# Dilated attention, product with V: V stationary instead of the probabilities, output turned back to rows by TensorE

## The chip, the cores and the metric

One program runs on one core of a Trainium2 chip. The metric is the device time of one execution in microseconds (us). The engines named below are TensorE (PE in the rows; its weight loads are PEld), VectorE (DVE), ScalarE (ACT), GpSimd (POOL) and SyncE (SP), which issues most of the loads. Lower is better.

## The reference, cut to what matters

The kernel computes two transformer-like blocks one after the other, for 1024 positions and 1024 features in float32. The change is in the second block, in its dilated attention: three groups of eight heads, each with its own stride between the positions that a query sees.

```python
DILATED_GROUPS = ((128, 1), (512, 4), (2048, 16))     # window, dilation
BLK, HEAD_DIM = 128, 64

def dilated_attention(q, k, v, window, dilation):
    ...
    qs = strided(q * (Dh ** -0.5))
    kb = with_prev(strided(k))          # own block of 128 keys and the one before
    vb = with_prev(strided(v))
    s = jnp.einsum('brnqhd,brnkhd->brnhqk', qs, kb, preferred_element_type=jnp.float32)
    ...
    m = jnp.max(s, axis=-1, keepdims=True)
    p = jnp.exp(s - m)
    den = jnp.sum(p, axis=-1)
    lse = m[..., 0] + jnp.log(den)
    o = jnp.einsum('brnhqk,brnkhd->brnqhd', p, vb.astype(jnp.float32))   # the product that changes
    o = o / jnp.swapaxes(den, -1, -2)[..., None]
    ...
    return o.astype(q.dtype), lse
```

## The kernel before

The kernel is a list of stages, each with a hand-written instruction sequence for every engine; semaphores (the `wait_ge` lines) order the engines against one another. Nothing reorders: what stands first in an engine's sequence runs first on it. The stage that is touched is `Dilated` (it fills the stretch from 1870 to 2480 us of the profiled execution).

It runs 12 units, i = 0 to 11. A unit is two heads of one group (group i % 3), with all 1024 positions in eight blocks of 128 queries, b = 0 to 7. A block looks at one or two chunks of 128 keys (`chunks`): in group 0 every block but the first has two, in group 1 the odd blocks have two, in group 2 all have one. Over the 12 units that makes 44 blocks with two chunks and 52 with one.

For a block, the work goes through the engines like this:

- `score` (PE, L2608 puts the mask in, L2610 adds the product of queries and keys, with 64 rows of the array for each head),
- `top` (DVE, L2503, the largest score of each row), `exps` (ACT, L2384, exponentials and their sums),
- `turn_p` (PE, L2627, transposes the probabilities of both heads, one or two chunks each), `take_turned` (ACT, L2394, copies them from PSUM to PT2),
- `value` (PE, L2639, the product with V into PSUM bank 7), `rows` (DVE, L2509 and L2512, row maximum and output to OS), `store` (POOL, L2447, to DRAM).

Into this are laid half tiles of the projection for the next units (`half_tile`, which calls `tile_part`: twelve matrix products of 128x512 at L319; in the last two units tiles of 24 products of 128x256 at L274). PE's order of one quarter q of a unit, with b = 2q, is: half tile; turn_p(b), score(b+2); half tile; **value(b), turn_p(b+1)**; half tile; **value(b+1), score(b+3)**, then for q < 2 the transposes of the next unit's V (`turn_v`, L2588), or for q >= 2 in every third unit those of a combined pair (`turn_pair`, L2273). Below, the first place in bold is called place A (48 times) and the second place B (48 times).

Other things that matter below: `v_rows` (ACT, L2369) copies the turned V out of the bank that turn_p(2) and turn_p(4) write next, so these wait for it; `pair_features` (ACT, L2279) does the same for the pair's bank, on which turn_p(6) waits in units 5, 8 and 11. In ACT's sequence both stand behind `exps(b+3)` and a split of weights (L258). DVE's sequence has `rows(b+1)` just ahead of `top(b+3)`. `value` of a block waits until DVE has copied the output of the block before, since there is one output place in PSUM.

`value` issues, for each head and chunk, one float32 product with the turned probabilities (128x128) as the stationary operand and V (128x64) as the moving one. Each is two instructions in the trace. The `Attention` stage of the first block (345 to 570 us) has a product of the other form, at L2123: V (64 columns) stationary, the turned probabilities (128 columns) moving, the two heads into the two halves of the output's partitions.

Of the kernel before, what the change touches and what calls it, by code (L numbers as in the profile page):

```python
# [16 lines left out]
F32 = mybir.dt.float32  # L17
# [3 lines left out]
ACT = mybir.ActivationFunctionType  # L21
AX = mybir.AxisListType.X

P = 128
# [3 lines left out]
HALF = 512  # L28
# [58 lines left out]
def hybrid_kernel(nc, A, out):  # L87
    ctx = ExitStack()
    with ctx:
# [42 lines left out]
        def phase(items):  # L132
# [49 lines left out]
        YC = phase([("below_yc", [P, 8, 512], F32), ("YC", [P, L], F32)])[1]  # L182
        (gv, XC, ct, cw, QR, KR, VF, PB2, V2, PT2, rt, rp, OS, mx2, mask_r) = phase(kept + [
            ("QR", [P, 2, L], F32), ("KR", [P, 2, L], F32),
            ("VF", [P, L], F32), ("PB2", [P, 2, 2, 256], F32),
            ("V2", [P, 2, 8, 2, HD], F32), ("PT2", [P, 2, 2, 2, P], F32),
            ("rt", [P, HALF], F32), ("rp", [P, HALF], F32), ("OS", [P, 2, 8, 2, HD + 2], F32),
            ("mx2", [P, 2, 16], F32), ("mask_r", [P, 4 * P], F32R)])
# [23 lines left out]
        gv_ready, gv_taken = sig("gate_v_tile_ready"), sig("gate_v_tile_taken")  # L212
        pair_loaded, pair_step, pair_exp = sig("head_pair_loaded"), sig("pair_step"), sig("pair_exponentials_ready")
        ct_turned, ct_taken = sig("combined_rows_turned"), sig("combined_features_taken")
        inverted, scale_rows, scale_taken = sig("row_sums_inverted"), sig("row_scales_spread"), sig("row_scales_taken")
# [109 lines left out]
        def first_tiles(pe, u, rows, ready):  # L325
# [4 lines left out]
            for half in range(2):  # L330
# [11 lines left out]
                for k in range(KT):  # L342
                    rows.turn(pe, half, k)
                    if k >= 2:
# [4 lines left out]
        compute_signals = [qk_ready, v_ready, v_turned, rotated, q_hi, q_lo, v_feat, v_taken, scores, maxima, probs, p_turned, p_taken,  # L349
                           values, rows_out, mask_made, gv_ready, gv_taken, pair_loaded, pair_step, pair_exp, ct_turned, ct_taken, inverted, scale_rows, scale_taken, rot, rope_step, rope_act, pe_a, pe_b, dve_a, dve_b, act_a, dv, ac, po, pe_s, d_in, d_in2, d_tab, d_gain, *x_pair,  # L350
                           pre_sum, sq_post, root_post, rec_post, sq_pre, root_pre, rec_pre, x_rows, rows_normed,
# [1801 lines left out]
        class Dilated(Stage):  # L2153
# [13 lines left out]
            def __init__(self, norm):  # L2167
                super().__init__()
                self.norm = norm
                n = self.N  # L2170
                self.u = take_units(2 * n + 2)
                self.gr, self.gt = gv_ready.take(16), gv_taken.take(16)
                self.xl, self.ps, self.px, self.ctt, self.ctk = self.take_pairs(3)
                self.qk_r, self.v_r, self.vt_r = qk_ready.take(4 * n), v_ready.take(2 * n), v_turned.take(2 * n)
                self.r, self.rs = rotated.take(4 * n), rot.take(12 * n)
                self.vf, self.vt = v_feat.take(2 * n), v_taken.take(2 * n)
                self.s, self.m, self.p = scores.take(16 * n), maxima.take(8 * n), probs.take(8 * n)
                self.t, self.pt = p_turned.take(8 * n), p_taken.take(8 * n)
                self.v, self.o, self.mk = values.take(8 * n), rows_out.take(8 * n), mask_made.take(1)
                self.stored = [x.take(64 * n) for x in d_dil]  # L2180
                self.ql = q_loaded.take(16 * n)
# [158 lines left out]
            def act(self, e):  # L2340
# [48 lines left out]
                def take_turned(i, b):  # L2389
# [4 lines left out]
                    nc.scalar.activation(PT2[:, b % 2, :, c:2, :], self.turned_p(c), ACT.Copy).then_inc(p_taken.sem, 1)  # L2394

                split_v(0)
                split_v(1)
# [9 lines left out]
                for i in range(self.N):  # L2407
                    qk, v = i + 1 < self.N, i + 2 < self.N
                    for q in range(4):
# [9 lines left out]
                        if q == 2 and self.pair_at(i, 1) is not None:  # L2419
                            self.pair_exps(e, self.pair_at(i, 1))  # L2420
                        gate_tile(i, 3 * q + 1)
                        take_turned(i, b + 1)
                        gate_tile(i, 3 * q + 2)
                        exps(i, b + 3)
                        if q == 0:
# [44 lines left out]
            def dve(self, e):  # L2470
# [35 lines left out]
                def rows(i, b):  # L2506
# [3 lines left out]
                                            None, ALU.mult)  # L2510
                    e.wait_ge(values.sem, self.v + 8 * i + b + 1)
                    nc.vector.tensor_copy(OS[:, i % 2, b, :, 0:HD], ps[:, 7, 0:P].rearrange("p (h n) -> p h n", h=2)  # L2512
                                          ).then_inc(rows_out.sem, 1)
# [37 lines left out]
            def pe(self, e):  # L2551
# [78 lines left out]
                def value(i, b):  # L2630
# [5 lines left out]
                    cs = self.chunks(i, b)  # L2636
                    for h in range(2):
                        for c in cs:
                            last = nc.tensor.matmul(ps[:, 7, h * HD:(h + 1) * HD], PT2[:, b % 2, h, c, :],  # L2639
                                                    V2[:, i % 2, b - 1 + c, h, :], start=c == cs[0], stop=c == 1)  # L2640
                    last.then_inc(values.sem, 1)

                first_tiles(e, self.qk_unit(0), self.norm, qk_ready)
# [10 lines left out]
                for i in range(self.N):  # L2654
# [9 lines left out]
                    for q in range(4):  # L2664
# [5 lines left out]
                        value(i, b)  # L2670
                        turn_p(i, b + 1)
                        half_tile(3 * q + 2)
                        value(i, b + 1)
                        score(i, b + 3)
                        if q < 2 and i + 1 < self.N:
                            turn_v(i + 1, q)
# [260 lines left out]
```

## Time and profile before

| | us |
|---|---|
| median of the runs (lowest, highest) | 3655.24 (3654.55, 3655.67) |
| the profiled execution, its own time | 3656.55 |
| its span, first to last instruction | 3654.6 |
| PE busy in the span | 3512.3 (96%) |
| DVE, ACT, POOL busy | 1421.5, 933.8, 987.5 |
| the Dilated stage | 1870 to 2480 |

The profiled execution lasts 1.95 us longer than its span and 1.31 us longer than the median. Busy PE time counts pipelined instructions that overlap, so how long a piece of work holds PE is read from the chain of waits, where each piece is counted from the end of the one before to its own end.

### The profile page before, as it was taken

The numbers are of one execution on the slowest core, as the hardware profiler recorded it, in microseconds if no ns is written. First come the engines' busy times: TensorE is split into PE (matmuls) and PEld (weight loads), VectorE is DVE, ScalarE is ACT, GpSimd is POOL, SyncE is SP. The second block draws the span as 40 slices with busy tenths as digits, with TensorE's granted clock in tenths as the row PEclk, the third lists the DMA queues.
The fourth block names the chain that finished last, engine by engine and source line by source line (L and its number), as shares of the span: only waits on it lengthen the run. The fifth ranks groups of instructions, "written<-read, shape, count | busy, mean of one in ns | idle before, by whom it ended". The sixth has DMA issues, their size and how long they took to land.

```text
span 3654.6 us, 44410 instructions
## 1 busy us (share of the span) xinstructions
PE 3512.3 (96%) x17467; PEld 2903.1 (79%) x17467; DVE 1421.5 (39%) x2268; ACT 933.8 (26%) x1575; POOL 987.5 (27%) x429
## 2 busy tenths in 40 slices
PE   7899999999998999999799999998999999999999
PEld 6688877888776888888678888887787778888887
DVE  6882452123345333333644455444113213122234
ACT  4233443312242111111333333333322221111112
POOL 1452102223214333333312222211323122332322
PEclk9999999999999999999999999999999999999999
DMA  4232012212221111111221212213122111111111
GB/s 130 59 85 85 19 52 72 66 52 75 104 81 52 46 57 46 46 46 46 69 85 47 64 46 64 65 45 110 52 75 98 46 52 47 46 56 47 46 46 58
DMA packets 203977, 226.86 MB, mean 62 GB/s; under 512 B 19224, under 2 KB 177604, under 8 KB 203340
## 3 DMA queue, kind: packets, MB, share of 16 engines
q1 hardware_dynamic: 178556, 169.85, 15.3%
q10 hardware_dynamic: 20912, 44.54, 3.5%
q0 software_dynamic: 4384, 10.74, 0.8%
q8 instruction: 87, 1.43, 0.2%
q14 instruction: 38, 0.31, 0.0%
HBM read 191.30 MB, written 31.69 MB: 61 GB/s over the span
## 4 chain that ended last, share of the span: by engine, by line
PE 86%; DVE 5%; issue 5%; POOL 2%; ACT 1%; DMA 0%; ACTq 0%; SPq 0%; DVEq 0%; POOLq 0%
PE ps L274 18%; PE ps L319 16%; PE ps L301 13%; PE ps L302 13%; PE ps L295 12%; PE ps L724 4%; PE ps L2639 2%; PE ps L2610 1%; POOL wlo L266 1%; PE ps L335 1%; PE ps L2627 1%; PE ps L2123 1%; DVE big L470 1%; PE ps L2104 1%; PE ps L500 1%
## 5 line engine op out<-in xcount | busy, mean ns | idle before, releaser
L266 POOL TENSOR_TENSOR wlo<-raw,whi 128x2048 fp32r<-128x2048 f32 (+1 forms) x162 | 700.6, 4325 | 1748.0 <-ACT whi L258 1747.2
L301 PE MATMUL ps<-h_lo,whi 128*128 128x512 f32 x1856 | 723.5, 390 | 2.1 <-POOL wlo L266 2.0
L302 PE MATMUL ps<-h_hi,wlo 128*128 128x512 f32 x1856 | 723.0, 390 | 0.0
L258 ACT ACTIVATE whi<-raw 128x2048 fp32r<-128x2048 f32 (+1 forms) x162 | 288.4, 1780 | 962.0 <-PE ps L295 597.8
L295 PE MATMUL ps<-h_hi,whi 128*128 128x512 f32 x1856 | 462.1, 391 | 9.1 <-DVE gu L2783 5.3
L295 PEld LDWEIGHTS ps<-h_hi,whi 128*128 128x128 f32 x1856 | 349.6, 189 | 83.0 <-issue 9.7
L301 PEld LDWEIGHTS ps<-h_lo,whi 128*128 128x128 f32 x1856 | 349.3, 188 | 76.0 <-POOL wlo L266 3.3
L302 PEld LDWEIGHTS ps<-h_hi,wlo 128*128 128x128 f32 x1856 | 349.0, 188 | 72.5
L1047 DVE TENSOR_TENSOR big<-big,ps 128x512 f32<-128x512 f32 x432 | 295.8, 687 | 252.1 <-PE ps L274 251.9
L274 PE MATMUL ps<-whi,f_hi 128*128 128x512 f32 x864 | 338.3, 392 | 21.8 <-POOL wlo L266 12.4
L319 PE MATMUL ps<-h_lo,whi 128*128 128x512 f32 x880 | 353.1, 401 | 3.9 <-POOL wlo L266 3.9
L319 PE MATMUL ps<-h_hi,wlo 128*128 128x512 f32 x880 | 345.8, 393 | 0.0
L274 PE MATMUL ps<-wlo,f_hi 128*128 128x512 f32 x864 | 337.6, 391 | 0.0
L274 PE MATMUL ps<-whi,f_lo 128*128 128x512 f32 x864 | 337.5, 391 | 0.0
L319 PE MATMUL ps<-h_hi,whi 128*128 128x512 f32 x880 | 230.6, 404 | 2.8 <-ACT VF L2364 2.8
L974 POOL TENSOR_TENSOR f_lo<-fv,f_hi 128x512 fp32r<-128x512 f32 x108 | 142.0, 1315 | 319.8 <-DVE f_hi L1038 319.8
L274 PEld LDWEIGHTS ps<-whi,f_hi 128*128 128x128 f32 x864 | 163.1, 189 | 58.0 <-issue 12.8
L319 PEld LDWEIGHTS ps<-h_lo,whi 128*128 128x128 f32 x880 | 166.1, 189 | 45.2 <-issue 5.7
L319 PEld LDWEIGHTS ps<-h_hi,wlo 128*128 128x128 f32 x880 | 166.3, 189 | 32.9
L319 PEld LDWEIGHTS ps<-h_hi,whi 128*128 128x128 f32 x880 | 159.5, 189 | 40.5 <-issue 4.5
L274 PEld LDWEIGHTS ps<-whi,f_lo 128*128 128x128 f32 x864 | 163.0, 189 | 34.1
L274 PEld LDWEIGHTS ps<-wlo,f_hi 128*128 128x128 f32 x864 | 163.1, 189 | 33.8
(330 smaller groups left out, 4613.1 us busy)
## 6 DMA issues: line engine op xcount, KB each, us to landing
raw<-in_w_ff_dram SPq DMA_DIRECT2D x32, 1024.0 KB, 5.2
raw<-in_w_in_dram SPq DMA_DIRECT2D x57, 512.0 KB, 4.6
raw<-in_w_in_dram SPq DMA_DIRECT2D x28, 1024.0 KB, 5.3
raw<-in_w_ffn_gate_dram SPq DMA_DIRECT2D x11, 1024.0 KB, 5.3
raw<-in_w_ffn_up_dram SPq DMA_DIRECT2D x11, 1024.0 KB, 5.2
raw<-in_w_ffn_down_dram SPq DMA_DIRECT2D x11, 1024.0 KB, 4.9
yt<-y_keep ACTq DMA_DIRECT2D x20, 512.0 KB, 3.9
raw<-in_w_out_dram SPq DMA_DIRECT2D x8, 1024.0 KB, 5.0
```

The source lines that it names most:

```text
L258: nc.scalar.activation(whi[c % 2][:, 0:cols], raw[c % 2][:, 0:cols], ACT.Copy).then_inc(s_hi.sem, 1)
L266: nc.gpsimd.tensor_tensor(wlo[c % 2][:, 0:cols], raw[c % 2][:, 0:cols], whi[c % 2][:, 0:cols].bitcast(F32), ALU.subtract).then_inc(s_lo.se ...
L274: last = nc.tensor.matmul(out_, lhs(a, k), rhs(b, k), start=(k == 0 and n == 0), stop=(k == ks - 1 and n == 2))
L295: first = nc.tensor.matmul(ps[:, bank + n, :], w(0, k, m * P, P), src[0][:, k, sl], start=k == 0, stop=False)
L301: nc.tensor.matmul(ps[:, bank + n, :], w(0, k, m * P, P), src[1][:, k, sl], start=False, stop=False)
L302: last = nc.tensor.matmul(ps[:, bank + n, :], w(1, k, m * P, P), src[0][:, k, sl], start=False, stop=k == ks - 1)
L319: x = nc.tensor.matmul(ps[:, bank, :], w(a, k, m * P, P), H[b][:, k, sl], start=j == 0, stop=j == 23)
L335: last = nc.tensor.matmul(ps[:, 2 * half + m, :], w(a, k, m * P, P), H[b][:, k, half * HALF:(half + 1) * HALF], start=(k == 0 and q == 0), ...
L724: last = nc.tensor.matmul(ps[:, t, :], H[a][:, 4 * (j % 2) + k, t * P:(t + 1) * P], w(b, k, 0, HALF), start=(j % 2 == 0 and k == 0 and q = ...
L974: nc.gpsimd.tensor_tensor(f_lo[:, c % 2, m, half * HALF:(half + 1) * HALF], fv[:, n % 2, :], f_hi[:, c % 2, m, half * HALF:(half + 1) * HA ...
L1047: nc.vector.tensor_tensor(dst, dst, ps[:, 4 + t % 4, :], ALU.add).then_inc(dve_b.sem, 1)
L2639: last = nc.tensor.matmul(ps[:, 7, h * HD:(h + 1) * HD], PT2[:, b % 2, h, c, :], V2[:, i % 2, b - 1 + c, h, :], start=c == cs[0], stop=c == 1)
```

## The change

`value` swaps its operands. V's 64 columns of a head become the stationary operand and the turned probabilities the moving one, and the loop over chunks is now outside that over heads, so that the two heads' products, which go to the two halves of the output's partitions, stand side by side. What comes out is features by positions. ACT copies it from PSUM to a new tile OF (`take_features`), PE transposes OF back to rows, into the next 128 columns of bank 7 (`rows` in PE's sequence), and DVE copies from there to OS as before.

```diff
+                def take_features(i, b):                                  # ACT
+                    e.wait_ge(values.sem, self.v + 8 * i + b + 1)
+                    nc.scalar.activation(OF[:, :], ps[:, 7, 0:P], ACT.Copy).then_inc(o_taken.sem, 1)
...
                         gate_tile(i, 3 * q + 1)
+                        take_features(i, b)
                         take_turned(i, b + 1)
                         gate_tile(i, 3 * q + 2)
+                        take_features(i, b + 1)
                         exps(i, b + 3)
...
-                    e.wait_ge(values.sem, self.v + 8 * i + b + 1)         # DVE, rows
-                    nc.vector.tensor_copy(OS[:, i % 2, b, :, 0:HD], ps[:, 7, 0:P].rearrange("p (h n) -> p h n", h=2)
+                    e.wait_ge(o_turned.sem, self.ot + 8 * i + b + 1)
+                    nc.vector.tensor_copy(OS[:, i % 2, b, :, 0:HD], ps[:, 7, P:2 * P].rearrange("p (h n) -> p h n", h=2)
...
-                    for h in range(2):                                    # PE, value
-                        for c in cs:
-                            last = nc.tensor.matmul(ps[:, 7, h * HD:(h + 1) * HD], PT2[:, b % 2, h, c, :],
-                                                    V2[:, i % 2, b - 1 + c, h, :], start=c == cs[0], stop=c == 1)
+                    for c in cs:
+                        for h in range(2):
+                            last = nc.tensor.matmul(ps[h * HD:(h + 1) * HD, 7, 0:P], V2[:, i % 2, b - 1 + c, h, :],
+                                                    PT2[:, b % 2, h, c, :], start=c == cs[0], stop=c == 1)
+                def rows(i, b):                                           # PE
+                    e.wait_ge(o_taken.sem, self.of + 8 * i + b + 1)
+                    nc.tensor.transpose(ps[:, 7, P:2 * P], OF[:, :], ident).then_inc(o_turned.sem, 1)
...
                         value(i, b)
                         turn_p(i, b + 1)
+                        rows(i, b)
                         half_tile(3 * q + 2)
                         value(i, b + 1)
                         score(i, b + 3)
+                        rows(i, b + 1)
```

Place A on PE, in unit 1, blocks 0 and 1, between the end of one half tile and the next. Before (PT is the turned probabilities, cst holds the identity, PB the probabilities):

```order
L2639 MATMUL ps<-V,PT 128x64 [waits output_rows_ready,v_rows_taken,turned_probabilities_taken]
L2639 MATMUL ps<-V,PT 128x64
L2627 MATMUL ps<-cst,PB 128x128 [waits turned_probabilities_taken,probabilities_ready]
L2627 MATMUL ps<-cst,PB 128x128 x3
L319 MATMUL ps<-h_hi,whi 128x512 [waits unit_hi_ready,v_features_ready]
```

And after:

```order
L2647 MATMUL ps<-PT,V 64x128 [waits output_rows_ready,v_rows_taken,turned_probabilities_taken]
L2647 MATMUL ps<-PT,V 64x128
L2635 MATMUL ps<-cst,PB 128x128 [waits turned_probabilities_taken,probabilities_ready]
L2635 MATMUL ps<-cst,PB 128x128 x3
L2653 MATMUL ps<-cst,OF 128x128 [waits output_features_taken]
L320 MATMUL ps<-h_hi,whi 128x512 [waits unit_hi_ready,v_features_ready]
```

The product is written to 64 partitions with 128 columns, and one transpose that waits for ACT stands between turn_p and the half tile. Place B on PE, just behind, as it is after the change:

```order
L2647 MATMUL ps<-PT,V 64x128 [waits output_rows_ready,turned_probabilities_taken]
L2647 MATMUL ps<-PT,V 64x128 x3
L2616 MATMUL ps<-mask_r 128x256 [waits probabilities_ready,tile_rotated]
L2616 MATMUL ps<-mask_r 128x256
L2618 MATMUL ps<-KR,QR 128x256 x2
L2653 MATMUL ps<-cst,OF 128x128 [waits output_features_taken]
L2596 MATMUL ps<-cst,VF 128x128 [waits turned_probabilities_taken,v_features_ready]
L2596 MATMUL ps<-cst,VF 128x128 x3
```

Here the new transpose stands behind the scores of block b+3 and ahead of turn_v; the rest of the order is the same. On DVE, at the same place, the copy keeps its place and changes what it waits for; before:

```order
L2509 TENSOR_SCALAR OS<-mx 128x2 [waits probabilities_ready]
L2512 COPY OS<-ps 128x2x64 [waits values_ready]
L2503 TENSOR_REDUCE mx<-ps 128x2 [waits scores_ready]
L2480 STREAM_SHUFFLE rp<-ps 128x512 [waits tile_rotated,qk_tile_ready]
```

and after:

```order
L2517 TENSOR_SCALAR OS<-mx 128x2 [waits probabilities_ready]
L2520 COPY OS<-ps 128x2x64 [waits output_rows_turned]
L2511 TENSOR_REDUCE mx<-ps 128x2 [waits scores_ready]
L2488 STREAM_SHUFFLE rp<-ps 128x512 [waits tile_rotated,qk_tile_ready]
```

The TENSOR_REDUCE (`top` of block b+3) is now queued behind a copy that waits for a transpose which PE issues after that block's scores.

## Rows read from the trace of the kernel before

**Rows 1.** The page: busy time by engine, and the chain's shares by engine.

```profile
PE 3512.3 (96%) x17467; PEld 2903.1 (79%) x17467; DVE 1421.5 (39%) x2268; ACT 933.8 (26%) x1575; POOL 987.5 (27%) x429
...
PE 86%; DVE 5%; issue 5%; POOL 2%; ACT 1%; DMA 0%; ACTq 0%; SPq 0%; DVEq 0%; POOLq 0%
```

**Rows 2.** The windows view of Dilated: busy us by engine, granted clock, DMA.

```profile
1870.00:2480.00 610.00, 599.82 (x3475) 498.23 (x3474) 275.66 (x547) 204.14 (x575) 136.49 (x122) 0.99 0.18 55
```

**Rows 3.** The chain, unit 0: start, length in us, what.

```profile
1890.33 0.84 PE ps L2639 x8
1891.17 0.29 PE ps L2608 x2
1891.46 0.63 PE ps L2610 x4
1892.09 0.59 PE ps L2588 x4
...
1895.43 0.12 issue
1895.55 0.63 PE ps L2627 x4
...
1909.16 0.44 PE ps L2627 x4
```

**Rows 4.** The chain, unit 2, where every block has one chunk.

```profile
2011.31 0.22 PE ps L2627 x2
2011.54 2.77 PE ps L319 x12
2014.31 0.39 PE ps L2639 x4
2014.70 0.23 PE ps L2608 x2
...
2015.35 2.95 PE ps L319 x12
```

**Rows 5.** The chain in Attention, products with V stationary (L2123).

```profile
468.83 0.37 PE ps L2123 x4
469.20 2.96 PE ps L319 x12
...
477.65 0.59 PE ps L2123 x8
...
486.62 0.37 PE ps L2091 x2
```

**Rows 6.** The chain: L2588 without a row-tiled product ahead.

```profile
1871.66 0.45 PE ps L2588 x4
```

**Rows 7.** The chain, unit 5: scores, DVE, ACT, then the waiting turn_p(6).

```profile
2162.47 0.02 issue
2162.49 0.43 DVE mx L2503
...
2165.63 0.49 ACT YC L2279
2166.11 0.14 issue
2166.25 0.41 PE ps L2627 x2
```

**Rows 8.** Groups of ACT and DVE, with shape: count, busy us, mean ns, idle.

```profile
L1939 ACT ACTIVATE RS<-ps 128x128 f32<-128x128 f32 x32 | 8.9, 277 | 7.1 <-PE ps L2112 5.8
...
L2512 DVE COPY OS<-ps 128x128 f32<-128x128 f32 x96 | 27.6, 288 | 100.4 <-PE ps L2639 100.4
```

**Rows 9.** The timeline of ACT and PE around a place A, unit 2.

```profile
1998.00 0.20 ACT L2384 ACTIVATION_READ_ACCUMULATOR PB<-ps,mx 128x1 f32 x1
2000.04 0.38 ACT L2394 ACTIVATE PT<-ps 128x256 f32<-128x256 f32 x1 [1.84 <-PE ps L2627]
...
1999.22 0.56 PE L2639 MATMUL ps<-V,PT 128*128 128x64 f32 x4
```

More of the change, by code:

```diff
@@ L182, in hybrid_kernel @@
         YC = phase([("below_yc", [P, 8, 512], F32), ("YC", [P, L], F32)])[1]
-        (gv, XC, ct, cw, QR, KR, VF, PB2, V2, PT2, rt, rp, OS, mx2, mask_r) = phase(kept + [
+        (gv, XC, ct, cw, QR, KR, VF, PB2, V2, PT2, rt, rp, OF, OS, mx2, mask_r) = phase(kept + [
             ("QR", [P, 2, L], F32), ("KR", [P, 2, L], F32),
@@ L186, in hybrid_kernel @@
             ("V2", [P, 2, 8, 2, HD], F32), ("PT2", [P, 2, 2, 2, P], F32),
-            ("rt", [P, HALF], F32), ("rp", [P, HALF], F32), ("OS", [P, 2, 8, 2, HD + 2], F32),
+            ("rt", [P, HALF], F32), ("rp", [P, HALF], F32), ("OF", [P, P], F32), ("OS", [P, 2, 8, 2, HD + 2], F32),
             ("mx2", [P, 2, 16], F32), ("mask_r", [P, 4 * P], F32R)])
@@ L213, in hybrid_kernel @@
         pair_loaded, pair_step, pair_exp = sig("head_pair_loaded"), sig("pair_step"), sig("pair_exponentials_ready")
+        o_taken, o_turned = sig("output_features_taken"), sig("output_rows_turned")
         ct_turned, ct_taken = sig("combined_rows_turned"), sig("combined_features_taken")
@@ L349, in hybrid_kernel @@
         compute_signals = [qk_ready, v_ready, v_turned, rotated, q_hi, q_lo, v_feat, v_taken, scores, maxima, probs, p_turned, p_taken,
-                           values, rows_out, mask_made, gv_ready, gv_taken, pair_loaded, pair_step, pair_exp, ct_turned, ct_taken, inverted, scale_rows, scale_taken, rot, rope_step, rope_act, pe_a, pe_b, dve_a, dve_b, act_a, dv, ac, po, pe_s, d_in, d_in2, d_tab, d_gain, *x_pair,
+                           values, rows_out, mask_made, o_taken, o_turned, gv_ready, gv_taken, pair_loaded, pair_step, pair_exp, ct_turned, ct_taken, inverted, scale_rows, scale_taken, rot, rope_step, rope_act, pe_a, pe_b, dve_a, dve_b, act_a, dv, ac, po, pe_s, d_in, d_in2, d_tab, d_gain, *x_pair,
                            pre_sum, sq_post, root_post, rec_post, sq_pre, root_pre, rec_pre, x_rows, rows_normed,
@@ L2179, in __init__ @@
                 self.v, self.o, self.mk = values.take(8 * n), rows_out.take(8 * n), mask_made.take(1)
+                self.of, self.ot = o_taken.take(8 * n), o_turned.take(8 * n)
                 self.stored = [x.take(64 * n) for x in d_dil]
```

## The prediction

> **What bounds the kernel now.** I read the page first: PE is busy for 96% of the span and holds 86% of the chain that ended last [rows 1]. Then the windows view of the stage that is touched, 1870 to 2480 us: PE is busy for 599.82 of 610 us, at a granted clock of 0.99 of full speed, while DVE, ACT and POOL work for 276, 204 and 136 us [rows 2]. So this stage is priced by what PE has in its queue, plus the places where PE waits. Last I read the chain itself, piece by piece: it shows how long each group holds PE, from end to end. The value product holds it 0.39 us for a block with one chunk (x4) and 0.84 us with two (x8) [rows 3, 4]. The reader is to see that the pieces follow one another without idle time, so any instruction added to PE here costs its full piece, and that in a few places the chain leaves PE and runs over DVE and ACT. Those are the places where a later release costs time.
>
> Two facts on PE's pieces carry the sum. A half tile (L319 x12) takes 2.77 us behind a product over the whole array, but 2.95 us behind the scores, which use 64 rows for each head [rows 4]. Likewise the four transposes of L2588 take 0.59 us behind the scores and 0.45 us elsewhere [rows 3, 6]. So a change in how the array is divided costs 0.14 to 0.2 us, paid by whatever comes next.
>
> **The products.** The new form is in the trace: L2123 has the same shapes (V's 64 columns stationary, 128 moving). It takes 0.37 us for x4 and 0.59 us for x8, and the half tile behind it takes 2.96 us in place of 2.77 [rows 5, 4]. Its pieces include the switch into the divided array; the switch out falls on the next piece. At both places what comes next is a short product over the whole array: turn_p at A, the mask product L2608 at B. For turn_p I take the 0.14 us of L2588. For L2608 I take L2091, the mask product of Attention, 0.37 us behind a divided array, against 0.23 us of L2608 now: 0.14 again [rows 5, 4].
> - One chunk: 0.37 + 0.14 - 0.39 = +0.12 us, 52 blocks: +6.2 us.
> - Two chunks: 0.59 + 0.14 - 0.84 = -0.11 us, 44 blocks: -4.8 us.
>
> Together +1.4 us. The pairing works (each further x4 costs 0.22 us where it cost 0.45), but the switches eat it. Bounds: the switch out between 0.05 and 0.24 us would make this -7 to +11 us.
>
> **The transposes of the output on PE, 96 of them.** One transpose in a row of them costs 0.11 us (0.22 for two, 0.44 for four) [rows 3, 4].
> - Place A: 48 x 0.11 = 5.3 us.
> - Place B: it stands behind the scores, so it pays 0.14 + 0.11 and frees what follows from the switch. Where L2588 follows (22 times) the net is 0.11 us; where a half tile or the like follows (26 times) it is 0.25 - 0.18 = 0.07 us. Sum 4.2 us.
>
> **The wait for ACT at place A.** At the end of a value product the way is now ACT copy, then transpose. ACT is free: in the row shown its last work before turn_p's copy ends at 1998.20, the value product starts at 1999.22 and ACT then idles 1.84 us in all [rows 9]; take_features fills that gap. A 128x128 copy out of PSUM takes 0.277 us on ACT [rows 8]. From the end of an ACT copy to the end of two waiting transposes the trace has 0.14 + 0.41 us [rows 7], for a single one 0.11 less, 0.44. So the rows are turned 0.02 + 0.28 + 0.44 = 0.74 us after the product. PE meanwhile has turn_p(b+1) and the transpose itself: 0.44 + 0.14 + 0.11 = 0.69 us where turn_p has four (32 places, groups 0 and 1) and 0.22 + 0.14 + 0.11 = 0.47 us where it has two (16, group 2). PE stalls 0.05 x 32 + 0.27 x 16 = 5.9 us. Bounds: 0 (the copy is seen earlier than I think) to 0.44 us at all 48, 21 us. At B the scores of b+3 (0.29 + 0.63 us with two chunks [rows 3], 0.23 us and more with one) cover the copy: nothing, and what would be paid without that cover is the same 0.44 us a block.
>
> **The chain over DVE and ACT.** DVE's output copy now waits for the transpose, which at B comes after the scores of b+3; `top(b+3)` is queued behind it, then exps(b+3), a split of weights and `v_rows` or `pair_features` on ACT, for which turn_p waits. That chain is already late: in unit 0 turn_p(2) takes 0.12 + 0.63 us in place of 0.44 [rows 3], and this repeats in each of units 0, 1, 3, 4, 6, 7, 9 (0.41 us in place of 0.22 in group 1); unit 10 has the same wait, longer. That makes 8 places. In units 5, 8 and 11 it is turn_p(6), through the combined pair [rows 7]. Today top starts 0.02 us after the scores [rows 7]. Afterwards it starts after the transpose (0.25 us), 0.02 us and DVE's copy of 0.288 us [rows 8]: 0.54 us later. The transpose's own net cost on PE is swallowed there, as PE waits anyway: 0.54 - 0.11 = 0.43 us more, 8 + 3 = 11 places, 4.7 us. In unit 11 the chain also goes from block 3's scores over a split on ACT and POOL to the next tile; there the +0.5 us takes the place of some 0.5 us that PE would lose at A, and nothing is added. Everywhere else the copies and top have a half tile (2.77 us) for cover. Bounds: 0 to 12 x 0.54 = 6.5 us.
>
> **The end of the stage.** The last block's output goes through ACT and PE before DVE can copy it, and the next stage waits for it: + 0.7 us. ACT gains 96 x 0.28 = 27 us of work beside 204 us in 610, which hides.
>
> **The sum**: 1.4 + 5.3 + 4.2 + 5.9 + 4.7 + 0.7 = 22.2 us. Against the profiled execution, 3656.55 + 22.2 = 3678.8 us; that one lasted 1.3 us longer than the median, so against the median 3655.24 + 22.2 = **3677.4 us**, 0.6% slower.
>
> **Rivals.**
> 1. *The switches cost nothing in the new places, and the products gain their full rate.* Then a block with one chunk takes 0.22 us and one with two 0.44 us: 52 x -0.17 + 44 x -0.40 = -26.4 us. If the wait at A is hidden as well, the other terms are 5.3 + 4.2 + 4.7 + 0.7 = 14.9 us, the net is -11.5 us, and the time **3644 us**, faster. With the wait at A as priced it is 3650 us, within 0.2%. It decides where in-and-out of the divided array costs under some 0.1 us a block. Against it: L2123 x4 takes 0.37 us and not 0.22, and the half tile behind it 2.96 us [rows 5]. The Trainium skill, "TensorEngine Tiling (Array Packing)", When to Use Tiling, advises exactly this swap for a moving dimension of 64 or less and gives up to 2x; its Key Properties say in turn that a change of tiling mode drains TensorE. By the first alone the result would be this rival's, and by the drain it would be my sum; the rows speak for the drain. Chance 0.04 for the faster form, 0.05 for the middle one.
> 2. *The switch out is cheap but not free* (0.05 us) and the wait at A is hidden: 22.2 - 8.6 - 5.9 = +7.7 us, **3663 us**. Chance 0.06.
> 3. *The wait for ACT is not covered at all*: if PE takes up weights ahead only as far as the waiting transpose, each A costs up to 0.44 us (21 us in place of 5.9) and some of B too: **3692 to 3700 us**. For it: after every wait in the trace the first transposes took 0.41 us for two in place of 0.22 [rows 7]. Against: turn_p's transposes stand ahead of it and need nothing from ACT's new copy. Chance 0.09.
> 4. *The change doesn't do what it says*: the two heads' products do not run side by side, so each further x4 costs the 0.45 us of today in place of 0.22, with the switches on top: 560 / 4 = 140 times 0.23 = 32 us more, **3709 us**. Against it stand the equal shapes of L2123 [rows 5]. Chance 0.02.
>
> **How the numbers follow.** My forecast has 0.74, the rivals the rest. 0.2% (7.3 us) is about what a measurement of this kernel can tell from no change. Faster by more: 0.04. Within: the middle case and part of rival 2, 0.07. Slower: 0.89. The range takes in the bounds of the unknown costs around 3677: down to 3664 (switches at the low bound, the stall at A hidden), up to 3694 (the stall at A in full); beyond it lie less than 2 in 10.
>
> **What would show each step.** In the chain of the changed kernel the value pieces should be 0.37 and 0.59 us, turn_p behind them 0.36 and 0.58 us, the mask product 0.37 us; L2123-like lengths without the longer successor would speak for rival 1. The single transpose should show as a piece of 0.11 us at A in groups 0 and 1, with some 0.3 us of ACT or issue ahead of it in group 2, and 0.25 us at B, with 2.77 us for the half tile behind it. In units 0, 1, 3, 4 and so on the chain should pass from the transpose to DVE's copy, top, exps, and the split. Group 2 should lose most per block with one chunk, and Attention and the feed-forward stages nothing. The forecast is wrong if PE's idle time in 1870 to 2500 us grows by over 15 us, or if the stage gets shorter.

## The result and the profile after

| | before | after |
|---|---|---|
| median, us (lowest, highest) | 3654.89 (3651.81, 3655.67) | 3674.62 (3673.50, 3675.40) |
| profiled execution, its own time | 3656.55 | 3673.50 |
| its span | 3654.6 | 3671.5 |
| the Dilated stage (below) | 605.3 | 624.6 |

The changed kernel is slower: the ratio of its time to that of the kernel before is 1.0057, with a 95% interval of 1.0044 to 1.0070. That is 19.7 us between the medians.

To see small effects I use the length of the stage itself in the profiled execution, from the start of ScalarE's first copy of turned V (1872.1 us before, 1870.1 after) to the start of VectorE's last output copy (2477.4 and 2494.7). It grew by 19.3 us. The 2 us by which the stage began earlier came about before it, in code that is the same in both; the medians don't show them (over all the runs below the stage begins between 1869.0 and 1873.7 us).

Part of the stage's length is chance, through TensorE's clock. PE has two long waits in it: 2.8 us ahead of the first half tile, and some 4 us in unit 11, where a tile waits for weights that ScalarE and GpSimd prepare. The half tile behind each of these waits ran, in the profiles before and after, in part at a granted clock of 0.50 (1.2 of 2.4 GHz), and how long that lasts differs from one execution to the next. In unit 11, before (L274) and after (L275):

```profile
2445.85 4.55 PE ps L274 x24
...
2459.92 4.97 PE ps L275 x24
```

The same tile takes 2.87 us elsewhere. The granted clock over these two pieces was 0.65 and 0.58. Over all the runs it took 4.43 to 5.49 us, and the first half tile 3.02 to 5.49 (5.41 before, 5.44 after). So I also give the stage without these two half tiles, and call that its steady part: 595.3 us before and 614.2 after. Of the 19.3 us, 18.9 are in the steady part and 0.4 are the clock.

The chain of waits in unit 2, after (start, length in us, what; "issue" is time in which the engine waited for nothing that the profile shows). Lines are numbered one to eight higher than before: L2647 is the product with V, L2635 turn_p, L2616 the mask, L2618 the scores, L2653 the new transpose, L2596 turn_v, L320 a half tile. It answers to [rows 4].

```profile
1999.69 0.37 PE ps L2647 x4
2000.07 0.37 PE ps L2635 x2
2000.43 0.01 issue
2000.44 0.33 PE ps L2653
2000.77 2.73 PE ps L320 x12
2003.51 0.37 PE ps L2647 x4
2003.88 0.37 PE ps L2616 x2
2004.24 0.42 PE ps L2618 x4
2004.67 0.26 PE ps L2653
2004.93 0.44 PE ps L2596 x4
```

The reader is to see what did not change and what did. The product itself is a little shorter (0.37 us in place of 0.39), but turn_p behind it takes 0.37 in place of 0.22, and the mask product 0.37 in place of 0.23: each pays for the array's return to the undivided form. At place A the transpose shows as 0.33 us, of which some 0.2 is waiting for ScalarE. At place B it takes 0.26 us, and the turn_v behind it gets back to 0.44.

The chain in unit 0, after, which answers to [rows 3]:

```profile
1888.52 0.59 PE ps L2647 x8
1889.10 0.43 PE ps L2616 x2
1889.54 0.63 PE ps L2618 x4
1890.17 0.27 PE ps L2653
1890.44 0.02 issue
1890.46 0.04 DVE OS L2520
1890.50 0.17 issue
1890.67 0.69 DVE mx L2511
...
1892.47 0.95 ACT whi L259
1893.42 0.49 ACT V L2371
1893.91 0.14 issue
1894.05 0.63 PE ps L2635 x4
...
1899.08 0.59 PE ps L2635 x4
1899.67 0.12 PE ps L2653
```

Here the chain leaves PE, as forecast: transpose, output copy, maxima, exponentials, the weight split, the V copy, then turn_p. Before, 4.09 us passed from the end of the scores to the end of turn_p(2) (1892.09 to 1896.18 in [rows 3]'s stretch: 0.59, 2.75, 0.12 and 0.63); now it is 4.51 us (1890.17 to 1894.68). The last two rows are a place A with two chunks: turn_p x4 covers the wait, and the transpose costs 0.12 us.

The view of who waited for whom in the stage, after (engine, line, releaser; total us, times, longest):

```profile
PEld ps L2653 <- ACT OF L2400: 4.5, 17, 0.6
PE ps L2635 <- ACT V L2371: 4.3, 8, 1.3
PE ps L2635 <- ACT YC L2281: 2.2, 3, 0.8
```

The first row's 17 times are the 16 places A of group 2 and the end of the stage; the other two are the 8 + 3 places of the chain over VectorE and ScalarE. The mean granted clock of the stage is 0.99 as before.

```profile
1870.00:2500.00 630.00, 615.60 (x3572) 467.75 (x3571) 276.56 (x547) 230.43 (x671) 136.45 (x122) 0.99 0.18 53
```

### The profile page after: what moved, and what is told of

It is laid out like the page before. It is cut to its first block, busy times and chain, and to the rows that moved or that the text cites. A ratio compares the mean times of both kernels' runs of the same rounds, so it can differ in the third digit from the quotient of the medians.

```text
span 3671.5 us, 44700 instructions
## 1 busy us (share of the span) xinstructions
PE 3525.8 (96%) x17563; PEld 2870.8 (78%) x17563; DVE 1424.4 (39%) x2268; ACT 960.1 (26%) x1671; POOL 986.9 (27%) x429
## 3 DMA queue, kind: packets, MB, share of 16 engines
q1 hardware_dynamic: 178556, 169.85, 15.1%
## 4 chain that ended last, share of the span: by engine, by line
PE 85%; DVE 5%; issue 5%; ACT 2%; POOL 2%; DMA 1%; ACTq 0%; DVEq 0%; POOLq 0%
PE ps L275 18%; PE ps L320 15%; PE ps L302 12%; PE ps L303 12%; PE ps L296 12%; PE ps L725 4%; PE ps L2618 1%; PE ps L2647 1%; POOL wlo L267 1%; PE ps L2635 1%; PE ps L336 1%; PE ps L2616 1%; PE ps L2124 1%; ACT whi L259 1%; DVE big L471 1%
## 5 line engine op out<-in xcount | busy, mean ns | idle before, releaser
L275 PE MATMUL ps<-whi,f_hi 128*128 128x512 f32 x864 | 338.6, 392 | 22.0 <-POOL wlo L267 12.4
L320 PE MATMUL ps<-h_lo,whi 128*128 128x512 f32 x880 | 352.0, 400 | 2.1 <-POOL wlo L267 2.1
L320 PE MATMUL ps<-h_hi,wlo 128*128 128x512 f32 x880 | 344.1, 391 | 0.0
L275 PE MATMUL ps<-wlo,f_hi 128*128 128x512 f32 x864 | 337.8, 391 | 0.0
L275 PE MATMUL ps<-whi,f_lo 128*128 128x512 f32 x864 | 337.6, 391 | 0.0
L320 PE MATMUL ps<-h_hi,whi 128*128 128x512 f32 x880 | 230.1, 404 | 2.8 <-ACT VF L2366 2.8
L275 PEld LDWEIGHTS ps<-whi,f_hi 128*128 128x128 f32 x864 | 163.1, 189 | 58.4 <-issue 12.8
L320 PEld LDWEIGHTS ps<-h_lo,whi 128*128 128x128 f32 x880 | 166.5, 189 | 40.8 <-issue 3.3
L320 PEld LDWEIGHTS ps<-h_hi,wlo 128*128 128x128 f32 x880 | 165.7, 188 | 32.6
L275 PEld LDWEIGHTS ps<-whi,f_lo 128*128 128x128 f32 x864 | 163.2, 189 | 34.2
L320 PEld LDWEIGHTS ps<-h_hi,whi 128*128 128x128 f32 x880 | 159.9, 190 | 38.4 <-ACT VF L2366 3.2
L275 PEld LDWEIGHTS ps<-wlo,f_hi 128*128 128x128 f32 x864 | 163.2, 189 | 33.7
```

The lines of the kernel that those rows point to most:

```text
L275: last = nc.tensor.matmul(out_, lhs(a, k), rhs(b, k), start=(k == 0 and n == 0), stop=(k == ks - 1 and n == 2))
L320: x = nc.tensor.matmul(ps[:, bank, :], w(a, k, m * P, P), H[b][:, k, sl], start=j == 0, stop=j == 23)
```

## The experiments

The theory is the sum of the prediction: the products gain what the switches of the array take back, and the loss is the turning of the output (transposes, one wait, one chain over two engines). The main rivals were that the turning is hidden and the switches lose all, or that a product's cost belongs to the block and not to the switch.

The runs were measured in several sessions, in which the kernel before had medians between 3653.6 and 3655.1 us. So each median stands beside that of the kernel before in its own session. All are in us, and differences in the text are taken before rounding:

| run | median (kernel before beside it) | stage | steady part |
|---|---|---|---|
| kernel before | | 605.3 | 595.3 |
| the change | 3674.62 (3654.89) | 624.6 | 614.2 |
| products alone | 3656.83 (3655.08) | 605.9 | 596.0 |
| turning alone | 3683.29 (3655.08) | 630.6 | 619.7 |
| change, heads outside | 3676.61 (3655.08) | 623.3 | 614.8 |
| products alone, one half | 3688.70 (3654.11) | 637.2 | 626.2 |
| change, maxima first | 3671.84 (3655.08) | 620.1 | 609.2 |
| before, copies first | 3650.71 (3653.63) | 599.9 | 590.8 |
| change, copies first | 3668.73 (3653.63) | 616.4 | 605.4 |
| change, transpose in the tile | 3673.47 (3653.63) | 621.6 | 611.6 |
| products alone, mask ahead | 3646.95 (3653.63) | 597.5 | 586.5 |
| before, copies first, mask ahead | 3649.77 (3653.93) | 600.1 | 589.1 |
| all four together | 3655.88 (3653.93) | 603.4 | 593.5 |
| paired | 3640.89 (3653.93) | 589.4 | 579.4 |

### The two halves of the change apart

Products alone. VectorE copies the features as they are:

```diff
-                        take_features(i, b)
-                        take_features(i, b + 1)
-                        rows(i, b)
-                        rows(i, b + 1)
-                    e.wait_ge(o_turned.sem, self.ot + 8 * i + b + 1)
-                    ... ps[:, 7, P:2 * P]
+                    e.wait_ge(values.sem, self.v + 8 * i + b + 1)
+                    ... ps[:, 7, 0:P]
```

> The changed product alone (V stationary, heads side by side); its features are neither copied by ScalarE nor turned back, and VectorE copies them to the output place as they are, so rows and features are left exchanged: the turning is left out. Theory (the sum): the products' pieces get 12.1 us shorter and the switches out of the divided array take about 14 us back, so the time is that of the kernel before within 3 us (+1.8 us). Rival (the products gain at their full rate and the +20 us are all the turning's): 12 to 26 us faster than the kernel before.

Measured: 3656.83 us against 3655.08, a ratio of 1.0003 (0.9993 to 1.0012); the stage takes 605.9 us against 605.3. The pieces are those of the changed kernel (0.37 and 0.59 us, mask 0.37, turn_p 0.37 and 0.59). So the swap by itself neither gains nor loses, and the rival of a full gain is out.

Turning alone, with the product in its old form:

```diff
-                    for c in cs:
-                        for h in range(2):
-                            last = nc.tensor.matmul(ps[h * HD:(h + 1) * HD, 7, 0:P], V2[...], PT2[...], ...)
+                    for h in range(2):
+                        for c in cs:
+                            last = nc.tensor.matmul(ps[:, 7, h * HD:(h + 1) * HD], PT2[...], V2[...], ...)
```

> The product in its old form (probabilities stationary, rows out), and still the copy by ScalarE and the transpose by TensorE, so the output comes out turned once too often: the two parts of the change apart, the second half. Theory: about 17 us slower than the kernel before: transposes 96 x 0.11 to 0.12 us, waits at the first place in blocks where turn_p is short (without the switch behind the product PE arrives 0.15 us earlier, so these waits grow to some 0.35 us in 16 blocks and 0.1 to 0.15 us in 32, 9 us instead of 3.5), the chain over VectorE and ScalarE 4 to 5 us, the end 1 us. At the second place the scores pay their own 0.2 us on what follows, as before. If the two parts were plainly additive it would be 20 minus 2, 18 us. Rival (the turning is hidden beside the tiles and the loss is from the switches): under 5 us slower.

Measured: 3683.29 us, a ratio of 1.0077 (1.0060 to 1.0094), 28 us slower than before and 8.7 us slower than the full change; the stage takes 630.6 us. The 17 us of the expectation were a slip of addition: its own parts (10.6, 9, 4 to 5, 1) make 25, and the stage grew by 25.3. The chain at a place A of group 2:

```profile
2002.43 0.41 PE ps L2647 x4
2002.84 0.02 issue
2002.86 0.29 ACT OF L2400
2003.15 0.04 issue
2003.19 0.33 PE ps L2653
2003.52 2.75 PE ps L320 x12
```

Here the way over ScalarE stands open: 0.02 + 0.29 + 0.04 + 0.33 = 0.68 us from the end of the product to the turned rows. And in the 32 blocks with a long turn_p the transpose takes 0.25 us, not 0.12. The two halves do not add: in the steady part the products alone make +0.6 us, turning alone +24.3 and both together +18.9. In the full change the 0.15 us by which the switch makes turn_p longer run while ScalarE copies, so the switch at A costs nothing there that the wait had not cost already: from the end of the product to the turned rows there are 0.71 us at A in the full change (0.37 + 0.34, or 0.59 + 0.12), and 0.68 to 0.69 here.

### Side by side: order, and halves of the array

```diff
-                    for c in cs:
-                        for h in range(2):
+                    for h in range(2):
+                        for c in cs:
```

> The changed kernel with the loop over heads outside that over chunks, as it was before: only the order of the products in the 44 blocks with two chunks differs. Theory (pairs overlap only where products of different halves of the array stand next to each other): the x8 pieces go from 0.59 to about 0.8 us in 44 blocks, 9 us slower than the changed kernel. Rival (the queue finds the pairs itself, or pairing is not what shortens the piece, only the 64-column weight load): the same as the changed kernel within 2 us.

Measured: 3676.61 us against 3674.62 for the change, within the scatter of both; the steady part of the stage is 0.6 us longer, where 9 us were expected, and the pieces are 0.37 and 0.59 as before. The theory on the order fell. Either TensorE finds the pairs itself, or they are not what makes the piece shorter. A run on top of the products alone decides between these two: both heads into the same half of the partitions.

```diff
-                            last = nc.tensor.matmul(ps[h * HD:(h + 1) * HD, 7, 0:P], V2[...], PT2[...], ...)
+                            last = nc.tensor.matmul(ps[0:HD, 7, h * P:(h + 1) * P], V2[...], PT2[...], ...)
```

> The products alone (as in the run without copy and turning), but both heads' features go to the same half of the partitions, side by side in the columns, so both use the same half of the array; the output is then not that of the reference in that part. Shapes, weight loads of 64 columns and switches are those of the products alone. Theory (what halves the growth of the piece is that two heads run at the same time in the two halves): each pair of instructions costs 0.22 us where it cost 0.11, x4 goes from 0.37 to about 0.59 us or somewhat under and x8 from 0.59 to about 1.0 us, 52 x 0.2 + 44 x 0.4 = 28 us slower than the products alone, about 3685 us. Rival (the shorter weight load alone does it, and a product costs 0.055 us wherever it stands): the same as the products alone, 3657 us.

Measured: 3688.70 us, a ratio of 1.0094 (1.0077 to 1.0111), 31.9 us slower than the products alone (30.2 in the steady part). From the chain, a block with one chunk and one with two (L2644 is the product with V here):

```profile
2005.75 0.58 PE ps L2644 x4
...
1901.28 1.02 PE ps L2644 x8
```

With the same shapes and the same weight loads the pieces grow from 0.37 to 0.58 us and from 0.59 to 1.02 us. So the two heads do run at the same time in the two halves of the array, and the order in which they are issued within a block does not matter.

### The chain over VectorE and ScalarE

The maxima ahead of the output copy on VectorE:

```diff
-                        rows(i, b + 1)
                         top(i, b + 3)
+                        rows(i, b + 1)
```

> The changed kernel with one exchange on VectorE: the row maxima of block b+3 are taken ahead of the output copy of block b+1, so the maxima do not wait for the turned rows. Theory (the chain over VectorE and ScalarE costs 0.3 to 0.4 us at 11 to 14 places): 4 to 5 us faster than the changed kernel, the waits of turn_p back at the kernel before's. Rival (that chain was late anyway and sets nothing): the same within 1.5 us.

Measured: 3671.84 us, 2.8 us faster than the change (ratio to before 1.0046, 1.0029 to 1.0063); the stage 620.1 us, 4.5 us shorter, its steady part 5.1. The stage bears out the theory; the medians alone, with intervals of some 6 us, could not.

The copies of V and of the pair ahead of the weight split on ScalarE, in the kernel before and in the changed one:

```diff
+                        if q < 2 and qk:
+                            v_rows(i + 1, q)
                         if q == 0:
                             if v:
                                 split_v(i + 2)
...
+                        if q >= 2 and self.pair_at(i, 2) is not None:
+                            self.pair_features(e, self.pair_at(i, 2), q - 2, 6)
                         if q == 2 and v:
                             split_qk(i + 2)
...
-                        if q < 2 and qk:
-                            v_rows(i + 1, q)
-                        if q >= 2 and self.pair_at(i, 2) is not None:
-                            self.pair_features(e, self.pair_at(i, 2), q - 2, 6)
```

> The kernel before with one exchange on ScalarE: the copy of the turned V rows (and of the combined pair's features) stands ahead of the weight split instead of behind it. Theory: the waits of turn_p(2) in 8 units (0.31 us in seven, more in unit 10) and of turn_p(6) in three units (about 0.3 us) vanish: 4 us faster than the kernel before. Rival (the split is then late for GpSimd and the tiles that need the low parts): no gain, or slower.

> The same exchange on ScalarE in the changed kernel. Theory: the chain over VectorE and ScalarE gets 1 us of slack at v_rows and 1.8 us at pair_features, so both the waits that were there before and the 0.4 us that the change added to each are gone: 7 to 8 us faster than the changed kernel, about 3667 us. Rival: only what the exchange gives the kernel before, 4 us.

Measured: the kernel before gets 2.9 us faster by the medians (3650.71 against 3653.63; ratio 0.9992, 0.9983 to 1.0001, so not clear of no change), its stage 599.9 us, 5.4 shorter. The changed kernel takes 3668.73 us; that is 15.1 us over the kernel before of the same session, where the change had 19.7 over its own. Its stage takes 616.4 us, 8.3 shorter. 0.9 us of the 5.4 is the clock, and the clock hid 0.5 us in the changed kernel: in the steady part the gains are 4.5 and 8.8 us. The difference, 4.2 us, is what the change had added to those waits, near the 4.0 us that the pieces give below. The chain in unit 0 of the changed kernel with this exchange no longer leaves PE:

```profile
1890.86 0.26 PE ps L2653
1891.12 0.44 PE ps L2596 x4
1891.56 2.75 PE ps L320 x12
1894.31 0.44 PE ps L2635 x4
```

### The wait at place A

The transpose behind the third product of the half tile, where ScalarE's copy is long done:

```diff
-                        rows(i, b)
-                        half_tile(3 * q + 2)
+                        half_tile(3 * q + 2, lambda: rows(i, b))
...
+                if mid and j == lo + 2:
+                    mid()
```

> The changed kernel with the transpose of the first place issued behind the third product of the half tile that follows, instead of ahead of it. Theory: the wait for ScalarE in group 2's blocks (0.22 us in 16 blocks, 3.5 us) is covered and vanishes, the transposes themselves stay at 0.11 us: 3.5 us faster than the changed kernel, and no idle time of TensorE on OF. Rival (a transpose in the middle of a running accumulation breaks the flow of weight loads): no gain or 2 to 5 us slower.

Measured: 3673.47 us, 1.2 us below the change's median and no nearer to the kernel before of its own session, so the medians show no gain. The stage takes 621.6 us, 3.0 shorter (2.7 in the steady part, of 3.5 expected). The chain in unit 2 shows the place (L2637 is turn_p here, L2655 the transpose):

```profile
2000.50 0.37 PE ps L2637 x2
2000.87 0.70 PE ps L320 x3
2001.57 0.11 PE ps L2655
2001.68 2.07 PE ps L320 x9
```

The transpose costs its 0.11 us inside a running accumulation and no more, and the wait is gone.

### What a change of the array's division costs

Products alone, and the mask product of block b+3 moved ahead of the product with V, so that the division by columns is followed directly by that by rows:

```diff
+                        score(i, b + 3, 0)        # the mask product
                         value(i, b + 1)
-                        score(i, b + 3)
+                        score(i, b + 3, 1)        # queries and keys
```

> The changed product alone, as in the run with the products only (no copy and no turning, so the output holds features where rows belong), and the mask product of block b+3 issued ahead of the product with V of block b+1 instead of behind it. The number of instructions is the same; at the second place the array is then divided by columns and right after by rows, one change of division less. Theory (every change of division costs 0.14 to 0.2 us): 48 x 0.14 = 6.7 us faster than the products alone, that is 3650 us, 5 us faster than the kernel before. Rival (the cost belongs to the product with V itself and not to the change of division): the same as the products alone.

Measured: 3646.95 us, a ratio of 0.9979 (0.9970 to 0.9988) to the kernel before, 9.9 us faster than the products alone (8.4 if each is taken against the kernel before of its own session); the stage 597.5 us, 8.5 shorter, its steady part 9.4. The chain in unit 2 (L2616 is the mask product, L2647 the product with V, L2618 the scores, L2593 turn_v):

```profile
1999.80 0.17 PE ps L2616 x2
1999.97 0.37 PE ps L2647 x4
2000.34 0.42 PE ps L2618 x4
2000.76 0.59 PE ps L2593 x4
```

The mask product takes 0.17 us in place of 0.37, and nothing behind it gets longer: the scores pay 0.42 us as ever. That is 0.20 us at a place (48 x 0.20 = 9.6 us), where I had expected 0.14. The control is the same move in the kernel before with its copies first, where the array stays undivided up to the scores:

> Control: the kernel before with its copies first (as above) and the mask product ahead of the product with V, in its old form, where the array is undivided at that point either way. Theory (the 9 to 10 us of the mask product ahead came from one change of division less): no gain here beyond 1 to 3 us from shorter weight loading between the pieces; a stage of 597 to 600 us against 599.8. Rival (moving the mask product ahead is itself worth 9 us): a stage of 591 us.

Measured: 3649.77 us, a ratio of 0.9988 (0.9978 to 0.9997), and a stage of 600.1 us against 599.9, just over the 597 to 600 expected. The clock hid a gain here: the steady part is 1.7 us shorter. So the move by itself gives a little where nothing is divided (the mask product falls from 0.23 to 0.17 us and from 0.29 to 0.24, while in group 2 the product behind it takes 0.44 us in place of 0.39). Of the 9.4 us with the divided product, 7.7 are left for the change of division: 0.16 us at each of the 48 places, near the 0.14 of the prediction.

### A version that beats both

All four arrangements together, with the two products of a quarter still apart, and then one with the products of b and b+1 next to each other, one copy of 128x256 and both transposes in the next half tile. OF is then twice as wide and lies in a part of the constants' tile that held masks which are no longer needed:

```diff
-                        value(i, b)
                         turn_p(i, b + 1)
                         half_tile(3 * q + 2)
+                        score(i, b + 3, 0)
+                        value(i, b)
                         value(i, b + 1)
-                        score(i, b + 3)
+                        score(i, b + 3, 1)
...
-                        half_tile(3 * q)
+                        half_tile(3 * q, (lambda: rows(i, b - 2)) if 4 * i + q else None)
...
+                    for t in range(2):
+                        last = nc.tensor.transpose(ps[:, 7, (2 + t) * P:(3 + t) * P], OF[:, t * P:(t + 1) * P], ident)
```

> The changed kernel with the copies first on ScalarE, the first place's transpose inside the half tile and the mask product ahead, and the two products of a quarter still apart. Theory: the gains add: 624.6 - 8.3 - 3.0 - 9.0 gives a stage of 604 us, equal to the kernel before within 2 us. Rival (they overlap, since a wait that is gone can't be won twice): a stage of 608 us or more.

> The changed product arranged to pay for one excursion out of the undivided array in a quarter where the changed kernel pays for two more: both blocks' products with V (b and b+1) stand together, behind the mask product of b+3 and directly ahead of its scores; one 128x256 copy on ScalarE and two transposes behind the third product of the next half tile; on VectorE the maxima ahead of the output copies; on ScalarE the V and pair copies ahead of the weight split. Nothing is left out. Theory, per quarter, from pieces of the runs so far: the products in one group save 0.15 us, no 0.15 us on turn_p, no 0.2 us between product and mask, transposes 0.22 us with no wait; from the stage of 616 us with the copies first: -7 -7 -10 -3, a stage of about 589 us against 605 before: 16 us faster than the kernel before, 3638 us. Rival (the product's cost belongs to the block and not to the switch, or the later products of block b delay something new on VectorE): 3648 us or more.

Measured: all four, 3655.88 us, a ratio of 1.0002 (0.9993 to 1.0012), stage 603.4 us against the 604 expected: equal to the kernel before. In the steady part the three gains (8.8, 2.7 and 9.4 us) add up to the 20.7 measured within 0.2 us. Paired: **3640.89 us**, where 3638 were expected, a ratio of 0.9962 (0.9948 to 0.9976), stage 589.4 us against 589 expected: 13 us faster than the kernel before, 33 to 34 us faster than the change. Its timeline on PE in unit 2 (L2621 is the mask product, L2652 the product with V, L2623 the scores, L321 a half tile):

```profile
2008.49 0.33 PE L2621 MATMUL ps<-mask_r 128*128 128x128 f32 x2
2008.75 0.66 PE L2652 MATMUL ps<-PT,V 128*64 128x128 f32 x8
2009.34 0.49 PE L2623 MATMUL ps<-KR,QR 64*128 64x128 f32 x4
2009.76 0.51 PE L321 MATMUL ps<-h_lo,whi 128*128 128x512 f32 x1
```

From start to start, the products of two blocks hold PE 0.59 us (2008.75 to 2009.34), where two blocks apart held it 0.37 + 0.37 and then 0.15 to 0.2 each for the way back.

## Why the prediction was right, point by point

The forecast was 3677 us with a range of 3664 to 3694; measured were 3674.6. The steps, each with what the pieces of the trace after give:

| step | forecast, us | measured, us |
|---|---|---|
| products and switches out | +1.4 | 52 x -0.02, 44 x -0.25, A 48 x 0.15, B 48 x 0.14: +1.9 |
| transposes at A | 5.3 | 48 x 0.12 = 5.8 |
| transposes at B | 4.2 | 22 x (0.26 - 0.15), 26 x (0.26 - 0.18): 4.5 |
| wait for ScalarE at A | 5.9 | 16 x (0.34 - 0.12) = 3.5 |
| chain over VectorE, ScalarE | 4.7 | 8 x 0.30, 3 x 0.30, 3 x 0.12, 0.35 in unit 11: 4.0 |
| end of the stage | 0.7 | 1.11 - 0.43: 0.7 |
| sum | 22.2 | 20.4 |

The stage grew by 19.3 us, of which 0.4 are the clock in unit 11 and 18.9 belong to the table. The largest part of the 1.5 us that the table has too much is the half tile behind place A: after the change it takes 2.75 us or a little less in place of 2.77, which makes 1.1 us over 48 places. No term has it. The rest is the rounding of the pieces.

- **The products.** Right to half a microsecond, since L2123 [rows 5] was the same operation. The piece lengths of 0.37 and 0.59, and 0.58/0.59, 0.36/0.37 for turn_p, came out as written. The products alone confirm it (+1.8 us by the medians). The price of a change of division at B held too: 0.14 us read as the longer mask product, 0.16 when one is avoided and the control is taken off (0.20 without the control).
- **The wait at A.** The term was too large by 2.4 us. I had taken 0.44 us from the end of ScalarE's copy to the end of a single transpose, from a turn_p that waited [rows 7]; it is 0.04 + 0.33 = 0.37 us (the run with the turning alone). The bound at which all 48 places pay in full was far off. So the 32 blocks with a long turn_p do not wait at all, and the 16 others wait 0.22 us and not 0.27.
- **The chain.** Right in its places and its order, too large in its size. The maxima started 0.50 us after the scores (0.27 + 0.02 + 0.04 + 0.17) and not 0.54, and the way from scores to turn_p grew by 0.42 us in unit 0 and by 0.47 in unit 5 (4.19 to 4.66 us, of which 0.05 is only that the scores' own piece ends earlier, 0.42 in place of 0.47). Less the transpose's own 0.11 that leaves 0.30 to 0.31 a place, where I had 0.43. On the other side, I had thought that group 2 has cover at turn_p(2); it has not quite (0.34 us in place of 0.22, in three units). And I had put the chain in unit 11, from block 3's scores over ScalarE and GpSimd to the next tile, at nothing, since it would take the place of a loss at A. No place A lies in that stretch: it comes after the tile that waits, pays in full, and the chain adds 0.35 us. Copies first, and maxima first, both gave back what turn_p had lost.
- **The end.** Right: from the end of the last half tile to VectorE's output copy there were 0.43 us before and there are 1.11 after. In the last unit ScalarE's copy of a gate tile (0.38 us) stands ahead of take_features, which I did not see, but it runs beside the product, which ends 0.04 us before take_features begins, so it costs next to nothing:

```profile
2493.61 0.38 ACT gv L2354
2494.00 0.28 ACT OF L2400
2494.28 0.04 issue
2494.32 0.34 PE ps L2653
2494.67 0.02 issue
2494.69 0.30 DVE OS L2520
```

- **The rivals.** The first needed switches at no cost, and the products alone put it out. Its source, the advice of the Trainium skill in "TensorEngine Tiling (Array Packing)", When to Use Tiling, is right about the rate (a further x4 costs 0.22 us and not 0.45; 0.44 when both heads use one half). The other sentence of the same page, in Key Properties, says that a change of tiling mode drains TensorE, and gives no price. That a change costs time agrees with the traces: 0.14 to 0.16 us each, which takes the gain away here as long as each block pays its own changes. The third, that nothing covers ScalarE's copy, is refuted by the 0.12 us transposes; the fourth, that the heads don't run side by side, by the run with both in one half, where each further x4 does cost 0.44 us.

That the sum came out so near owes something to errors of both signs: the wait and the chain were 3.1 us too large and the first three steps 1.3 us too small, and the shorter half tile behind A had no term.

## What to carry to other kernels

What a divided array costs goes by the number of times that it is divided and undivided again, not by the number of products: gather what runs in divided form (here both blocks' products and the scores) into one group. Every change of division cost 0.14 to 0.2 us, while a further product in divided form cost 0.11 (x4 is two products). When a change adds a hop over another engine, look at what is queued behind the instruction that now waits (here the maxima behind the output copy) and at which chains are late already; put the hop's last step into the middle of a long piece of work, where it cost 0.11 us and no wait. Two halves of a change need not add: the longer turn_p hid a wait, and turning alone was 8.7 us slower than turning with the swap.

## What the runs showed of the hardware that I had not expected

TensorE overlaps the products of the two halves of the array whatever their order within a block (0.59 us for x8 with heads inside or outside). A division by columns followed directly by one by rows costs no more than the one change that the scores pay anyway (mask product 0.17 us, then 0.37 and 0.42). That is 0.20 us less than with an undivided product between them, of which the control gives 0.04 to the move itself.

The wait of 2.8 us ahead of the stage's first half tile is the same in all 14 traces, and what the clock does behind it is not. In 13 of them the granted clock stood at 0.50 for part of that half tile, which took 4.41 to 5.49 us; in one, the change with heads outside, it stayed at 1.00, and the half tile took 3.02 us. A difference of a microsecond or two between single profiles of this kernel can be that alone.
